# A decoder step whose sparse attention is selected and attended in pairs of tiles, partly between norm steps

## What is computed

```python
proj = rmsnorm(x, g_pre) @ w_in                      # q, k, v, indexer q/k/weights, u
score = sum_h relu(qi_h . ki) * wi_h                 # indexer, causal
idx = top_k(score, 256)                              # per query
a_o = softmax(q . k[idx]) @ v[idx]                   # 8 heads, 2 KV heads, head size 64
s_o = glu(s5_scan(u))                                # state-space half
mix = concat(a_o, s_o) @ w_out
x = x + rmsnorm(mix, g_post)
x = x + rmsnorm(square(relu(rmsnorm(x, g_ffn_pre) @ w_up)) @ w_down, g_ffn_post)
```

## Time and profile before

| | us |
|---|---|
| median of the three timed runs | 3682.56 |
| lowest and highest | 3680.38, 3683.88 |
| the profiled execution | 3676.49 |
| its span, first to last instruction | 3674.8 |
| mean granted TensorE clock | 0.912 of full speed |
| PE, PEld busy | 3039.5, 2401.7 |
| DVE, ACT, POOL busy | 1842.5, 1637.8, 1244.2 |

### The profile page before, as it was taken

One profiled execution on the slowest core, in us unless ns is written; L12 is line 12 of the kernel. 1 busy time (PEld: TensorE's weight loads), 2 busy tenths in 40 slices (PEclk: granted clock), 3 DMA queues, 4 the chain that ended last, 5 costly groups with the idle time before them and its releaser, 6 DMA issues.

```text
span 3674.8 us, 47108 instructions
## 1 busy us (share of the span) xinstructions
PE 3039.5 (83%) x15352; PEld 2401.7 (65%) x15352; DVE 1842.5 (50%) x4116; ACT 1637.8 (45%) x2873; POOL 1244.2 (34%) x1149
## 2 busy tenths in 40 slices
PE   7998544647778889996799999968999999699996
PEld 5886421314556668764577886646778888588885
DVE  4432962762357984367685332666772333511112
ACT  3332412522546755575563446745634444322222
POOL 1332620313013561253264114522672112224444
PEclk9999766868879999998899999889999999899998
DMA  4444344546336564354454223343543213544443
GB/s 152 138 140 151 86 128 131 136 133 205 102 130 216 207 248 134 116 200 146 164 182 166 82 79 122 128 171 120 184 165 114 70 61 129 188 146 152 174 154 111
DMA packets 219182, 529.45 MB, mean 144 GB/s; under 512 B 57514, under 2 KB 114924, under 8 KB 192924
## 3 DMA queue, kind: packets, MB, share of 16 engines
q1 hardware_dynamic: 199900, 499.65, 39.6%
q0 software_dynamic: 9824, 18.40, 1.6%
q10 hardware_dynamic: 9216, 8.39, 0.7%
HBM read 399.43 MB, written 134.12 MB: 145 GB/s over the span
## 4 chain that ended last, share of the span: by engine, by line
PE 49%; DVE 12%; issue 10%; ACT 5%; POOL 3%; DMA 3%; SPq 1%; ACTq 1%; POOLq 0%; DVEq 0%
PE r L1620 16%; PE r L1652 12%; PE po L1700 4%; PE tr L1691 3%; ACT junk_a_b L1969 2%; POOL acc_b L2104 1%; PE sc L1668 1%; PE sc L1679 1%; PE sc L1678 1%; PE r L1809 1%; DVE junk_v_b L2343 1%; DVE trial_b L2295 1%; PE tr L1668 1%; PE r L1765 1%; POOL hr_b L2085 1%
## 5 line engine op out<-in xcount | busy, mean ns | idle before, releaser
L2104 POOL TENSOR_TENSOR acc_b<-acc_b,part_b 128x512 f32<-128x512 f32 x375 | 516.1, 1396 | 495.8 <-ACT part_b L1920 494.9
L1652 PE MATMUL r<-ready_b,h_b 128*128 128x512 f32 x2304 | 569.4, 403 | 42.2 <-ACT part_b L1920 38.2
L1652 PEld LDWEIGHTS r<-ready_b,h_b 128*128 128x128 f32 x2304 | 437.4, 193 | 159.2 <-ACT part_b L1920 50.7
L1620 PE MATMUL r<-x_hi_b,ready_b 128*128 128x512 f32 x1536 | 493.6, 395 | 5.4 <-DVE x_lo_b L2209 2.8
L2085 POOL TENSOR_TENSOR hr_b<-hr_b 128x512 f32<-128x512 f32 x128 | 148.4, 1159 | 777.1 <-ACT hr_b L1907 776.8
L1969 ACT ACTIVATE junk_a_b<-score_b,trial_b 128x384 int8<-128x384 f32 (+13 forms) x266 | 347.5, 1306 | 103.5 <-DVE trial_b L2295 102.4
L1620 PEld LDWEIGHTS r<-x_hi_b,ready_b 128*128 128x128 f32 x1536 | 290.8, 189 | 75.8 <-issue 10.1
L1920 ACT ACTIVATE part_b<-r 128x512 f32<-128x512 f32 x390 | 223.5, 594 | 217.1 <-PE r L1652 130.8
L1700 PEld LDWEIGHTS po<-V_sb,pT_b 128*128 128x128 f32 x2176 | 287.5, 192 | 23.1 <-issue 3.1
L1620 PE MATMUL r<-x_lo_b,ready_b 128*128 128x512 f32 x768 | 301.0, 392 | 0.0
L1996 ACT ACTIVATE pT_b<-tr 128x512 f32<-128x512 f32 (+3 forms) x320 | 168.8, 527 | 264.4 <-PE tr L1691 262.6
(11 more groups left out here) (407 smaller groups left out, 6028.6 us busy)
## 6 DMA issues: line engine op xcount, KB each, us to landing
ready_b<-ws_u SPq DMA_DIRECT2D x96, 1024.0 KB, 6.7
ready_b<-ws_d SPq DMA_DIRECT2D x96, 1024.0 KB, 5.0
ws_u<-up_b SPq DMA_DIRECT2D x32, 1024.0 KB, 8.8
ws_d<-dn_b SPq DMA_DIRECT2D x30, 1024.0 KB, 6.5
raw_b<-w_out SPq DMA_DIRECT2D x64, 256.0 KB, 3.2
raw_b<-w_up SPq DMA_DIRECT2D x32, 512.0 KB, 5.5
raw_b<-w_down SPq DMA_DIRECT2D x32, 512.0 KB, 4.1
kv_b<-kv_pages SPq DMA_DIRECT2D x96, 128.0 KB, 3.8
```

Source lines behind the costliest of these rows:

```text
L1620: mm = pe.matmul(x[:], wt[:, c], y[:, k], start=k == n == 0, stop=(k, n) == (KD - 1, 2))
L1652: mm = pe.matmul(x[:], f[:, tok], w[:, col], start=c == n == 0, stop=(c, n) == (KQ - 1, 2))
L2104: pool.tensor_tensor(dst, dst, part[:, add_no[key] % 2, :], ALU.add).then_inc(add_pool, 1)
```

## The change

Tiles 4 to 7 stay one lot. Tiles 8 to 15 become four lots of two, each selected and then attended. `n_bank`, `ahead`, `last_of` and SP's waits and loads are written for lots of any length. `between_norms` lists the part of a group ahead of its first up chunk: behind the last W unit it puts the begin of an attention, and behind each of the 40 M and N units that follow some of its steps, 36 in all (`NORM_STEPS`). Group 1 opens with the lot of tiles 8, 9, group 2 with that of 12, 13. The rest is merged: in group 0 the selection and attention of tiles 4 to 7 and the selection of 8, 9; in group 1 the rest of that attention, selection and attention of 10, 11 and the selection of 12, 13; in group 2 the rest, and selection and attention of 14, 15. `merge` takes its factor as an argument: 1.02, and 1.2 in group 2. The whole diff:

```diff
--- before.py
+++ after.py
@@ -801,8 +801,9 @@
     part_w = lambda w, size, b: min(size, w - size * b)
 
 
-    SELECT = ((2, 3), (4, 5, 6, 7), (8, 9, 10, 11), (12, 13, 14, 15))
-    ATTEND = tuple(tuple(range(4 * s, 4 * s + 4)) for s in range(4))
+    SELECT = ((2, 3), (4, 5, 6, 7), (8, 9), (10, 11), (12, 13), (14, 15))
+    ATTEND = ((0, 1, 2, 3), *SELECT[1:])
+    lot_of = {t: ts for ts in ATTEND for t in ts}
     pieces = lambda t: [(h, u) for h in range(NIH) for u in range(halves(t))]
     piece_step = lambda p: 1 if p == 0 else 2
 
@@ -814,8 +815,8 @@
             out += [(("S", s, p, k), 0.5 if p == 0 else 1.0 + w * 1.1e-3) for k in range(n)]
         return out
 
-    n_bank = lambda s: 4 * NH * (s + 1)
-    ahead = lambda s: s + 2
+    n_bank = lambda s: len(ATTEND[s]) * NH * banks(ATTEND[s][0])
+    ahead = lambda s: banks(ATTEND[s][0]) + 1
 
     def attend_units(s):
         return [(("AB", s), 8.0)] + [(("A", s, j), 0.5) for j in range(-ahead(s), n_bank(s) + 6)]
@@ -855,8 +856,8 @@
         at += [(2 * T - 2, ("F", g, T - 1), 0.0)] * (g == NG - 1)
         return out + [(u, c) for _, u, c in sorted(at, key=lambda x: (x[0], x[1][0] != "D", x[1][2]))]
 
-    def merge(main, side):
-        whole, share = sum(c for _, c in main), sum(c for _, c in side) * 1.04
+    def merge(main, side, early=1.04):
+        whole, share = sum(c for _, c in main), sum(c for _, c in side) * early
         out, a, b, i = [], 0.0, 0.0, 0
         for u, c in main:
             out.append(u)
@@ -872,13 +873,34 @@
     for u in merge(first_side[14:], samples[1:]):
         plan += [u] + [("GL", u[1] - 1)] * (u[0] == "SF" and 1 <= u[1] <= N_GATE)
     plan += [("B",)]
-    late = [u for s in range(1, 4) for u in select_units(s) + attend_units(s)]
-    plan += merge([u for g in range(NG - 1) for u in feed_units(g)], late)
-    ended = []
-    plan += [u for u, _ in ended + feed_units(NG - 1)] + [("Z",)]
+
+    def between_norms(g, side):
+        main, out, n = [u for u, _ in feed_units(g)], [], 0
+        turns = {u: i for i, u in enumerate(u for u in main[:main.index(("U", g, 0))] if u[0] in "MN")}
+        for u in main[:main.index(("U", g, 0))]:
+            out.append(u)
+            if u[0] == "W" and u[2:] == (1, nt(g) - 1):
+                out.append(side[0][0])
+                n = 1
+            elif u in turns and n:
+                m = 1 + NORM_STEPS * (turns[u] + 1) // len(turns)
+                out += [v for v, _ in side[n:m]]
+                n = max(n, m)
+        return out, side[n:]
+
+    NORM_STEPS = 36
+    rest_of = lambda g: feed_units(g)[[u for u, _ in feed_units(g)].index(("U", g, 0)):]
+    plan += merge(feed_units(0), select_units(1) + attend_units(1) + select_units(2), 1.02)
+    for g, s in ((1, 2), (2, 4)):
+        mixed, left = between_norms(g, attend_units(s))
+        plan += mixed
+        left += select_units(s + 1) + attend_units(s + 1)
+        plan += merge(rest_of(g), left + select_units(s + 2), 1.02) if g == 1 else merge(rest_of(g), left, 1.2)
+    plan += [u for u, _ in feed_units(NG - 1)] + [("Z",)]
     place = {u: n for n, u in enumerate(plan)}
-    for g in range(1, NG):
-        assert place["A", g, n_bank(g) + 5] < place["D", g - 1, ND - 2, 0]
+    for s, ts in enumerate(ATTEND):
+        if s:
+            assert place["A", s, n_bank(s) + 5] < place["D", ts[0] // 4 - 1, ND - 2, 0]
     feed = [u for u in plan if u[0] not in ("S", "A", "AB", *SAMPLE)]
     is_last = lambda u: u[2] == nt(u[1]) - 1 and u[3] == 0
     queued = [u for u in feed if u[0] not in "ME" or is_last(u)]
@@ -1059,9 +1081,9 @@
                     bank_of[s, j] = t, h, b
                     n, j = n + 1, j + 1
     m = 0
-    last_of = lambda t: NH * (t // 4 + 1) * (t % 4 + 1) - 1
+    last_of = lambda t: NH * banks(t) * (lot_of[t].index(t) + 1) - 1
     tile_at = lambda s, j: next((t for t in ATTEND[s] if last_of(t) == j), None)
-    for s in range(4):
+    for s in range(len(ATTEND)):
         for j in range(n_bank(s) + 6):
             if (s, j) in bank_of:
                 turn_no["p", *bank_of[s, j]] = m
@@ -1465,7 +1487,7 @@
                     if p == 0 and k == 0:
                         if s:
                             for i in range(2):
-                                sp.wait_ge(aT_st[i], 16 * 2 * s)
+                                sp.wait_ge(aT_st[i], 16 * (ATTEND[s][0] // 2))
                         load_index(ts[0])
                         load_index(ts[1])
                     if 1 <= p and k == 0 and p + 1 < len(ts):
@@ -1478,13 +1500,13 @@
 
                 def attend_step(s, j):
                     if j > 0 and (s, j) in bank_of and bank_of[s, j][1:] == (0, 0):
-                        if bank_of[s, j][0] % 4 < 3:
+                        if bank_of[s, j][0] < ATTEND[s][-1]:
                             load_mask(bank_of[s, j][0] + 1)
                     if (s, j + ahead(s)) in bank_of:
                         t, h, b = bank_of[s, j + ahead(s)]
-                        if (h, b) == (QPK, 0) and t % 4 < 3:
+                        if (h, b) == (QPK, 0) and t < ATTEND[s][-1]:
                             load_query(t + 1, 0)
-                        if (h, b) == (0, 0) and t % 4:
+                        if (h, b) == (0, 0) and t > ATTEND[s][0]:
                             load_query(t, 1)
                     if tile_at(s, j - 5) is not None:
                         store_output(tile_at(s, j - 5))
@@ -1554,9 +1576,9 @@
                         for i in range(2):
                             sp.wait_ge(mask_st[i], 16 * (n // 2))
                         for kv in range(NKV):
-                            load_query(4 * u[1], kv)
+                            load_query(ATTEND[u[1]][0], kv)
                         for t in range(2):
-                            load_mask(4 * u[1] + t)
+                            load_mask(ATTEND[u[1]][t])
                     elif u[0] == "A":
                         attend_step(*u[1:])
                     elif u[0] == "Z":
```

## The result

The changed kernel takes **3766.43 us** (median of 4 runs, 3761.69 to 3767.95); the kernel before took 3681.47 us beside it (3679.53 to 3683.88). The ratio is 1.0228, interval 1.0211 to 1.0246: slower by 85 us. The forecast was 3693 us, range 3645 to 3738, with the most of the chance on slower: the side was the likelier one, the size was missed by 73 us, and the time lies above the range.

A forecast was written before the change was run, and what follows sets the result against it. TensorE, 49% of the chain, was taken as the bound, VectorE in group 0's selection windows, with idle openings to fill. Groups at +26, -4 and -11 gave +11 on 3676.5; with the median 6.1 above, 3693 us, range 3645 to 3738.

The forecast's parts named there:

- I take 7 us from the last projection to the first useful score: Openings of groups 1 and 2: TensorE's wait for queries and masks, 7 us within an opening of 72.
- end of 14: Upper end of the 7 us wait at an opening: 14 us if the masks land last.
- 36 x 1.57 = 56.5: Filled openings: 36 attention steps at 1.57 us each, the step cost where a lot fills, 56.5 us.
- Each more lot loads its indices behind the attention's last store, 3 to 5 us: Restarts of the selection: each additional lot costs 3 to 5 us, included in the group sums.
- Group 0, +26: Group 0 with denser search ticks and the whole selection of tiles 8, 9: 712 us against 686.1.
- VectorE is the bound: Group 0's selection windows of 21, 20 and 19 ticks: 69.0, 60.2, 52.0 us with VectorE busy 56.5, 55.8, 49.5.
- the end of the group 18 us, which is short since only two ticks are left there: End of group 0: 18 us, with only two search ticks left there.
- What the pairs cost and the placing gives: Groups 0 to 2: +47 us for the pairs less 36 for filling the openings, +11 in sum.
- the 3 us twice: Openings of groups 1 and 2: filled, they run at 2.4 GHz by the clock rule, some 3 us back each; sum 3687.
- the opening is throttled: Slower rival: at the openings VectorE stands at a mask's landing and blocks every engine; 95 for 72 us, 3739; chance 0.13.
- Packing costs little: Faster rival: packed selection runs at the best windows' pace; terms fall by 18, 20 and 8 us, 3647; chance 0.35.
- The placing doesn't overlap: Slower rival: masks land only after the norm chain, opening 27.3 + 56.5, 12 us lost twice, 3717; chance 0.08.

The follow-up runs named there:

- b_qi: The kernel before the change, with index queries of the next lot's first tile loaded early into memory of their own: 3669.25 us (0.9978).
- a_early_qi: The changed kernel with the openings' queries and masks loaded ahead of the ready weights, and index queries loaded early for restarts: 3709.83 us (1.0084).
- a_unplaced: The changed kernel with the attention of tiles 8, 9 and 12, 13 behind the norm steps instead of between them: 3768.46 us (1.0248).

## Why the prediction was wrong, step by step

- **"I take 7 us from the last projection to the first useful score"** failed. The queries landed 7.0 us after the last projection, as said, but the first score is useful only when its mask is there, and masks landed last: 13.4 us to the first transposed probability. The step had named this as its end of 14 and chose 7 because it looked at TensorE's wait alone. VectorE's and its queue's wait of 17.61 us was the one that counted. Loading both early took 12.6 and 8.3 us off the openings (89.1 and 84.8 to 76.5).
- **"36 x 1.57 = 56.5"** was too cheap in a place full of roots: 14 table loads an opening are 9.0 and 7.4 us. The 1.57 came from a window without a norm in it. Without roots and late loads, 67.5 and 69.1 us stand against my 64.5 without the 7 us of stall.
- **"Each more lot loads its indices behind the attention's last store, 3 to 5 us"**: the waits were near that (2.1 to 4.8), their price was not. The four restarts cost 24 us together, 2.3 to 9.8 each, for waits of 14.5 us, with the matmuls behind a wait at a lower clock. That is all of the 9 us missed in the window behind group 2's opening (103.6 us with early index queries, against 104), and 6 of the 18 in group 1's: there 83.5 us stay against 72, and TensorE alone is busy 77.6 of them, so the term held too little work. Which part it lacked is open.
- **Group 0, +26**: measured +21.7, with the second to fourth window at 74.6, 63.4 and 53.4 for 77, 67 and 51. But its reason, **"VectorE is the bound"**, did not come out of the windows that it was read from: with the lower counts cut, b_qi's second window goes from 69.1 to 68.2 us, for 4.5 us less of VectorE's work, and its third from 60.1 to 57.1, neither towards 50. And **"the end of the group 18 us, which is short since only two ticks are left there"** failed: 25.8, and 27.4 for 17 in group 1, with the mask's choosing in front of a norm step.
- **What the pairs cost and the placing gives**: my terms held +47 (26, and 14 and 7 with the 18 of the placing added back) and -36. Measured, with early loads, +71 and -30. The pairs' 24 us more stand in group 1: 23, 48 and 9 us by group, where my terms were 26, 14 and 7. What I had left out there is TensorE's waits for copies, relus and queries.
- **The clock in the openings.** The filled openings were granted 0.81 and 0.88, not full speed. Behind the 7 us of waiting it was 0.50 and 0.66 (1776 to 1782, 1782 to 1790 us), and it fell again to 0.55 (1800 to 1810) and 0.66 (1830 to 1840), where TensorE waits for no transfer. Without the wait (a_early_qi) it is 0.87 and 0.91, and in the version without late loads and roots 0.92 and 0.93. So the 3 us twice that the prediction worked out beside the Trainium skill ("TensorE: Matmul & The Clock Gate", on the clock gate) did not come back in the kernel as built.
- Of the **rivals**, "the opening is throttled" named the mechanism that came: VectorE standing at a mask's landing with the norm queued behind it. Its opening of 95 us was nearer than my 72; its time of 3739 missed because the restarts and the dearer windows of groups 1 and 2 were not in it. I gave it 0.13, on the ground that the steps of four tiles are interleaved; interleaving does not help a queue whose head is a wait. "Packing costs little" is refuted by 71 us. "The placing doesn't overlap" (3717) was true in its outcome for the kernel as built, by the 2 us between it and a_unplaced, but not by its mechanism: the first mask was there 9.8 us into the opening, not at the end of the norm chain.

The ledger: the forecast was +11, 47 for the pairs less 36 for the placing. Measured beside these runs it is +88 (3766 for 3678.5). The late transfers cost 57, of which the kernel before pays 9 too; the tables cost 17; the pairs cost 71 and not 47; and the placing, with its inputs early and no tables, gives 47 and not 36. That the version without late transfers and tables takes 3693 us, the forecast's own number, is luck: the 9 us that the kernel before would save too are off it, and the errors of 24 and 11 partly cancel. The late transfers, at the openings and the restarts, are 48 us of the 77 missed: the largest step that failed.

## What to carry to other kernels

When work is moved into a gap, follow each of its inputs through the queue it is issued on: 128 KB behind 5 MB arrives with the 5 MB, and the engine that stands at it blocks its whole queue. Load the small things first or earlier; that alone made the kernel before 1% faster, with no work moved at all. Before mixing two kinds of work on ScalarE, list their functions, and price a short wait of TensorE at more than its length (here 1.7 and 2.1 times). And look at where a packed stretch ends: what stands last in one engine's queue delays what the next stage needs first.

## What the runs showed that I had not expected

- A wait of 4.5 us for DMA cost 9.5 us: the clock granted over the stretch rose from 0.83 to 0.94 when it was taken away, and the same 224 matmuls were busy 5.9 us less. Over the changed kernel's four restarts, 24 us went with waits of 2.1, 4.8, 3.6 and 4.0 us. The Trainium skill ("TensorE: Matmul & The Clock Gate", on how the clock oscillates in kernels) describes matmul bursts slowed by waits for DMA between them; the rows agree, and put the price of the 4.5 us wait at its own length again.
- A table load is 1.28 us of ScalarE, and its neighbours stand close, as in a_early_qi's opening:

```profile
1757.77 1.28 ACT L1913 ACT_TABLE_LOAD   x1
1759.07 0.20 ACT L1913 ACTIVATE root_b<-mean_b 128x1 f32<-128x1 f32 x1
1759.18 0.58 ACT L2027 ACTIVATE pT_b<-tr 128x512 f32<-128x512 f32 x1
1759.77 1.28 ACT L2033 ACT_TABLE_LOAD   x1
```

The kernel paid 0.6 us for each of the 28. The Trainium skill ("ScalarE: Activation LUTs", on what a load costs) adds a drain that makes it about 2.7 us; 0.02 us behind the load the next instruction starts here, so the measurement decides for 1.28.
